# A hybrid attention, SSM and mixture-of-experts step on one core: coefficient tables and rotations built at other places on VectorE, GELU in four blocks, two of five output tiles summed on TensorE

## The reference

```
h = rmsnorm(x);  q, k, v, u = split(h @ w_in)
a = sink_attention(q, k, v)                 # window 128; streams read a cache
abar, bbar = discretise(a_re, a_im, log_dt, b)      # complex, 32 groups x 64 states
h_t = abar * h_(t-1) + bbar u_t;  y = Re(C h) + d u
y = gelu(y);  y = y * sigmoid(y @ w_glu + b_glu)
x = x + concat(rmsnorm(a), rmsnorm(y)) @ w_out
f = rmsnorm(x);  x = x + sum over 2 chosen of 32 experts of gate * swiglu_e(f)
out = rmsnorm(x, g_final)
```

## Time and profile before

| | |
|---|---|
| median of 3 runs | 891.31 us (889.7 to 893.34) |
| the profiled execution | 890.42 us |
| its span, first to last instruction | 888.2 us |
| outside the span | 2.2 us |
| mean granted TensorE clock | 0.918 |
| PE, DVE, ACT, POOL busy share | 86%, 36%, 24%, 19% |

### The profile page before, as it was taken

How to read it: one execution, slowest core, us unless ns; L and a number is a source line. 1 busy time by engine, 2 the same in 40 slices (tenths; PEclk the granted TensorE clock), 3 DMA queues, 4 the chain that set the end, 5 groups by cost and what they waited for, 6 DMA issues and landing times.

```text
span 888.2 us, 15231 instructions
## 1 busy us (share of the span) xinstructions
PE 766.0 (86%) x5066; PEld 482.6 (54%) x5067; DVE 319.6 (36%) x754; ACT 214.0 (24%) x445; POOL 168.3 (19%) x380
## 2 busy tenths in 40 slices
PE   5999977799999993899998878888999999999840
PEld 3555555557554553566664444445666666666520
DVE  3478699760225335222211111111222122222117
ACT  4000244500422221122221211212222222222113
POOL 2006003300002001322222212222222222222110
PEclk9999988995789995899998999999999999999885
DMA  8202153180772439799999999999999968999955
GB/s 350 84 0 100 41 61 68 14 225 10 227 308 67 170 152 397 280 419 414 418 416 420 416 419 417 419 419 418 418 413 397 416 251 349 417 419 416 416 208 247
DMA packets 59617, 255.76 MB, mean 288 GB/s; under 512 B 19850, under 2 KB 22794, under 8 KB 36368
## 3 DMA queue, kind: packets, MB, share of 16 engines
q1 hardware_dynamic: 52560, 242.86, 69.8%
q0 software_dynamic: 6240, 11.46, 3.5%
q10 hardware_dynamic: 768, 0.72, 0.2%
HBM read 241.38 MB, written 22.30 MB: 297 GB/s over the span
## 4 chain that ended last, share of the span: by engine, by line
PE 59%; DMA 17%; SPq 10%; DVE 8%; ACT 3%; issue 2%; POOLq 0%; POOL 0%; DVEq 0%; ACTq 0%
PE pair L957 15%; PE pair L979 12%; DMA slot<-in_w_exp_down 10%; PE pair L753 7%; PE pair L616 6%; SPq L334 4%; PE pair L958 3%; DMA kv_row<-in_w_exp_down 3%; DMA slot<-in_w_in_qkv 2%; SPq L337 2%; PE pair L858 2%; PE pair L931 2%; PE pair L678 2%; PE pair L617 2%; SPq L325 2%
## 5 line engine op out<-in xcount | busy, mean ns | idle before, releaser
L958 PE MATMUL pair<-slot,probs 128*64 128x256 f32 x800 | 178.6, 382 | 0.0
L1603 DVE TENSOR_TENSOR sums<-iota_t,sums 128x640 bf16<-128x640 f32 x38 | 32.0, 841 | 286.4 <-POOL sums L547 280.3
L957 PE MATMUL pair<-slot,probs 128*64 128x256 f32 x576 | 129.1, 383 | 5.9 <-issue 3.3
L979 PE MATMUL pair<-slot,sums 128*64 128x512 f32 x400 | 100.7, 648 | 16.1 <-DMA slot<-in_w_exp_down 12.9
L958 PEld LDWEIGHTS pair<-slot,probs 128*64 128x64 f32 x800 | 110.2, 138 | 0.0
L957 PEld LDWEIGHTS pair<-slot,probs 128*64 128x64 f32 x576 | 79.4, 139 | 45.0 <-issue 12.9
L616 PE MATMUL pair<-reg_h,slot 128*128 128x512 f32 x160 | 84.0, 607 | 4.0 <-DMA slot<-in_w_in_qkv 2.2
L958 PE MATMUL pair<-reg_f,probs 128*64 128x256 f32 x384 | 84.9, 380 | 0.0
L531 POOL DMA_INDIRECT y_scr<-sums,y_now x40 | 42.8, 1070 | 189.8 <-ACT sums L1175 132.3
L523 POOL DMA_INDIRECT probs<-hf_scr,row_u x38 | 40.1, 1056 | 202.8 <-DMA y_scr<-sums,y_now 106.0
L957 PE MATMUL pair<-reg_h,probs 128*64 128x256 f32 x352 | 77.9, 379 | 0.3 <-DMA slot<-in_w_exp_up 0.3
(11 more groups left out here) (367 smaller groups left out, 1089.6 us busy)
## 6 DMA issues: line engine op xcount, KB each, us to landing
slot<-in_w_exp_up SPq DMA_DIRECT2D x22, 2048.0 KB, 24.2
slot<-in_w_exp_down SPq DMA_DIRECT2D x44, 1024.0 KB, 24.5
slot<-in_w_exp_gate SPq DMA_DIRECT2D x16, 2048.0 KB, 27.4
reg_f<-in_w_exp_up SPq DMA_DIRECT2D x10, 2048.0 KB, 25.4
reg_h<-in_w_exp_gate SPq DMA_DIRECT2D x8, 2048.0 KB, 26.8
reg_x<-in_w_exp_gate SPq DMA_DIRECT2D x8, 2048.0 KB, 28.6
reg_h<-in_w_exp_down SPq DMA_DIRECT2D x10, 512.0 KB, 23.1
reg_f<-in_w_exp_down SPq DMA_DIRECT2D x10, 512.0 KB, 21.8
```

Source lines behind the costliest of these rows:

```text
L957: pe.matmul(gu[j][0:TT], lhs, gate_w[g][:, h, c, out], start=n == 0, stop=n == KD - 1)
L958: ins = pe.matmul(gu[j][TT:P], lhs, up_w[q][:, h, c, out], start=n == 0, stop=n == KD - 1)
L979: ins = pe.matmul(yp[TT * h:TT * h + TT], hid_t[:, k, :], down_w[q][k][:, 512 * h:512 * h + 512], start=k == 0, stop=k == KH - 1)
L1603: tt(sel, iota_t[:].unsqueeze(1).to_broadcast([P, NT, P]), place_of[:, 0].unsqueeze(2).to_broadcast([P, NT, P]), ALU.is_equal)
```

## The change

Five edits, all in the order or the place of work; what is computed stays the same.

1. **VectorE, early.** `proj_out(0)` to `proj_out(5)` are moved later in VectorE's program, and the powers and step tables so come earlier. `out_table(0)` is made right after the step tables (in two parts, with `probs` as scratch), and `rotations(0, 4)` right after `masked(0)`.
2. **VectorE, in the loop.** `rotations(4, 6)` moves from turn 1, behind `masked(3)`, to turn 0, ahead of `proj_out(7)`. `out_table(1)` moves from turn 3 to turn 1, behind `masked(3)`, in four parts with 1024 columns of `slot[0]` as scratch. `out_table(0)` leaves turn 2. That scratch is later written by `bp_copy`, so ScalarE waits for `out_tab_done` ahead of those copies.
3. **Streams on VectorE.** The input halves (`stream_in`) of groups 0 and 1 run ahead of the output half of group 0, and so on.
4. **GELU.** ScalarE runs both remaining stream copies, `pt_copy(9)` and `pt_copy(10)`, ahead of GELU, and GELU in four blocks of 640 columns; TensorE's gate product waits for one block at a time.
5. **Tail.** VectorE makes four diagonal 128x128 matrices of the gates. TensorE adds tiles 1 and 3 in PSUM: the identity times the residual, plus each diagonal times its `got` rows. ScalarE and VectorE then read these two tiles from PSUM. VectorE adds tiles 0, 2 and 4 as before; the steps stand in another order.

The core of the diff:

```diff
-            proj_out(0)
...
             for n, (x, y) in {2: (1, 1), 3: (2, 1), 4: (2, 2), 5: (4, 1), 6: (4, 2), 7: (4, 3), 8: (4, 4)}.items():
                 cmul(power(n), power(x), power(y), (pv(12), pv(14)))
-                if n == 5:
-                    proj_out(2)
+                if n == 3:
+                    proj_out(0)
+            proj_out(1)
...
             dve.wait_ge(s["in_small"], 48)
+            out_table(0, probs[:].rearrange("p b n -> p (b n)"))
+            proj_out(5)
             masked(0)
+            rotations(0, 4)
             kv_rows()
...
+                if n == 0:
+                    rotations(4, 6)
                 if n < 3:
                     proj_out(7 + n)
                 if n + 2 < 8:
                     masked(n + 2)
-                if n == 0:
-                    rotations(0, 4)
-                elif n == 1:
-                    rotations(4, 6)
+                if n == 1:
+                    out_table(1, spare)
+                    dve.sem_inc(s["out_tab_done"], 1)
...
-                if n in (2, 3):
-                    out_table(n - 2)
```

```diff
+            stream_in(0)
+            stream_in(1)
+            stream_out(0)
+            stream_in(2)
+            stream_out(1)
+            stream_out(2)
...
-            act.wait_ge(s["y_in"], 16)
-            act.activation(y_g, y_t, ACT.Gelu_apprx_tanh).then_inc(s["gelu_done"], 1)
             pt_copy(9)
             pt_copy(10)
+            act.wait_ge(s["y_in"], 16)
+            for b in range(GB):
+                act.activation(y_g[:, b], y_t[:, b], ACT.Gelu_apprx_tanh).then_inc(s["gelu_done"], 1)
```

```diff
+            pe.wait_ge(s["diag_done"], 1)
+            pe.wait_ge(s["resid_back"], 16)
+            for i in by_pe:
+                for h in range(2):
+                    pe.matmul(by_pe[i][:, 512 * h:512 * h + 512], ident[:], resid[:, i, 512 * h:512 * h + 512],
+                              start=True, stop=False)
+            for n, i in enumerate(by_pe):
+                pe.wait_ge(got_in[i], 16)
+                for h in range(2):
+                    for k in range(2):
+                        ins = pe.matmul(by_pe[i][:, 512 * h:512 * h + 512], dg[:, n, k],
+                                        got[i][:, k, 512 * h:512 * h + 512], start=False, stop=k == 1)
+                ins.then_inc(s["summed"], 1)
...
             dve.wait_ge(s["resid_back"], 16)
-            for i in range(NT):
+            add_rows(0)
+            mean_square(0)
+            final_norm(0)
+            for i in range(2, NT, 2):
                 add_rows(i)
-                if i >= 1:
-                    final_norm(i - 1)
+                mean_square(i - 1)
+                final_norm(i - 1)
                 mean_square(i)
-            final_norm(NT - 1)
+                final_norm(i)
```

More of the change, by code:

```diff
@@ L102, in build @@
         x_t = reg_h[:].rearrange("p (k t) -> p k t", k=KD)
-        out_tmp = [reg_h[:, 2048 * i:2048 * i + 2048].rearrange("p (r t c) -> p r t c", r=R, t=T) for i in range(2)]
+        spare = slot[0][:, 2560:3584]
         states = reg_h[:, 0:2560].rearrange("p (r i n) -> p r i n", r=R, i=2)
@@ L208, in build @@
         down_w += [[reg_h[:, 4096:5120], reg_f[:, 4096:5120], probs_t[:], kv_f[:, 0:D]]]
+        pp = [ctx.enter_context(nc.psum_tensor(f"pair{i}", [P, 2, 512], F32)) for i in range(4)]
+        pp_sum = [pp[1][:].rearrange("p b n -> p (b n)"), pp[2][:].rearrange("p b n -> p (b n)")]
         xrow = probs[:, 0, 0:512]
@@ L1304, in _ @@
             dve.sem_inc(s["bbar_done"], 1)
-            proj_out(3)
+            proj_out(2)
             def step_table(i):
@@ L1348, in out_table @@
                           for n in range(2)]
-                c1, c2 = out_tmp
-                tt(c1, (cr, ci)[i], ar, ALU.mult)
-                step(tt(c2, (ci, cr)[i], ai, ALU.mult))
-                step(tt(out_tab[:, :, i], c1, c2, (ALU.add, ALU.subtract)[i]))
+                n = tmp.shape[1] // (2 * R * GC)
+                c1, c2 = tmp.rearrange("p (x r t c) -> p x r t c", x=2, r=R, t=n)[:, 0], \
+                    tmp.rearrange("p (x r t c) -> p x r t c", x=2, r=R, t=n)[:, 1]
+                for t in range(0, T, n):
+                    part = lambda x: x[:, :, t:t + n]
+                    tt(c1, part((cr, ci)[i]), part(ar), ALU.mult)
+                    step(tt(c2, part((ci, cr)[i]), part(ai), ALU.mult))
+                    step(tt(part(out_tab[:, :, i]), c1, c2, (ALU.add, ALU.subtract)[i]))
             def kv_rows():
@@ L1497, in _, with stream_in @@
             op_out(1)
-            for j in range(3):
+            def stream_in(j):
                 nb = min(3, NB - 3 * j)
```

36 lines of the change are left out of this document (22 added, 14 removed).

## The result

| | before | after |
|---|---|---|
| median of 4 runs each | 890.85 us (889.70 to 893.34) | 881.37 us (880.52 to 882.36) |
| ratio, 95% interval | | 0.9877 (0.9846 to 0.9907) |
| the profiled execution, its span | 890.42, 888.2 us | 880.52, 878.8 us |
| repeated beside 29 runs of before: mean of 10 | 893.15 us | 884.81 us, ratio 0.9905 (0.9876 to 0.9934) |

Forecast were 886.3 us and a range of 883.8 to 890.5; the change brought more than that, 9.5 us at first and 8.3 when repeated. The ratios in this document are the recorded ones; they are not the quotients of the medians or means beside them, and differ from these by up to 0.2%. I cut both traces at five points that stand in every kernel: four starts in TensorE's program, `scores(0)`, the first product of `out_project`, the first sample scores and the first gate (GLU) product, and VectorE's first add of the tail.

The account below looks back on a forecast made before the run. TensorE held 59% of the end's chain, DMA 17%, VectorE 8%; front -2.5, GELU -0.5 and tail -2.0 made -5.0 on 890.42, 885.4, or 886.3 us against the median, range 883.8 to 890.5.

Parts of the forecast that it names:

- Streams and GELU: Sample products: TensorE's 0.51 us wait for copies behind GELU goes, -0.5 us, bounds -0.5 and +0.5; reordered halves bring nothing.
- The cover that I named for GELU behind the copies: At the gate product: GELU's first block ready at 248.9 us, ahead of TensorE's need, with 1 us of cover.
- Front: Mixing part up to scores(6): moved tables and rotations remove the wait ahead of turn_probs(3), -2.5 us, bounds -4.2 and -0.5.
- The bound of -4.2: Largest gain allowed ahead of scores(6), with TensorE's clock staying full through weighted(1) and chunk_sums.
- `kv_rows` no longer waits for TensorE: Sign of a wrong forecast in VectorE's early part: it would mean that part is overfull; about 1 us of waiting was expected left.
- `ssm_out`'s clock changed: Sign of a wrong forecast: TensorE's clock in the SSM's output products was expected to stay as before.
- From `scores(6)` at 149.30 on, each engine waits as before, shifted: Step behind the early mixing part: what is gained by scores(6) is kept, with later waits unchanged.
- Tail: From VectorE's first add to the end: two pairs of adds go to TensorE, -2.0 us, bounds -2.15 and +2.2.
- Rival (b): Tail: TensorE stays at 1.2 GHz, 2.08 us a product, tail ends 2.2 us later than before; 890.5 us or less, chance 0.12.
- (a): Front: GpSimd's later clearing meets masked(5) and costs it 3.3 us, so the front yields nothing; 888.8 us, chance 0.14.
- (d): Front: clock falls in gaps at 121 to 130 us, stays low to chunk_sums' end; +6.2 us, 897.5, chance 0.05.
- The rule on transposes: Turning in the front: transposes don't count as TensorE activity in the same way, so the clock would stay low through it.

Follow-up runs that it names:

- after_again: The changed kernel run once more with no edit; mean 884.81 us, ratio 0.9905 to the kernel before.
- front_only: The kernel before with only the moved tables, rotations and early output drains on VectorE; mean 889.93 us, ratio 0.9976.
- tail_only: The kernel before with only the new tail, two tiles summed by TensorE; mean 890.97 us, ratio 0.9972.
- no_streams: The changed kernel with GELU and VectorE's sample order put back as before; mean 886.76 us, ratio 0.9920 to the kernel before.
- no_front: The changed kernel with tables, rotations and early drains put back as before; mean 886.64 us, ratio 0.9935 to the kernel before.
- best1: The changed kernel with tables, rotations and drains as before and GpSimd's conv_w clearing moved behind the states; mean 885.28 us, ratio 0.9925 to the kernel before.
- clear_later: The kernel before with one line moved, GpSimd clearing conv_w behind the states; mean 891.74 us, ratio 0.9991.

## Why the prediction was wrong

By the means of four traces each the change brought 7.1 us where the sum had 5.0: 2.1 more in streams and GELU, 0.5 more in the tail, 1.2 less in the front, and 0.7 in stages that it doesn't act on.

**Streams and GELU, the step that failed.** "-0.5 us", with bounds of -0.5 and +0.5, was the wait of one execution, 0.51 us, taken for the size of the thing. The wait is what is left between two moving times: `y_t` from DRAM plus 3.1 us for GELU and two copies, and TensorE's arrival, which depends on its clock. It was short in that trace since TensorE ran at 0.57 over 233 to 241 us. Over nine traces it ran from none to 4.95 us, and the clock stayed low longer behind the long ones: some 7 us behind waits of up to 0.5 us, some 10 behind those of about 2 to 3, some 14 behind the two above 4. The part is worth 2.6 us in the mean of these traces, 7.3 in the one pair with the full clock. No rival held this, and the earlier trace rows with the clock of 233 to 241 us would have pointed to it: `out_project`'s last part would be 1.9 us shorter at the full clock (3.60 in the trace of after, not 5.46), the landing where it was, hence some 1.9 us more wait. The cover that I named for GELU behind the copies held, 0.9 us in `after_again` where I said 1: no block made TensorE wait.

**Launch, not in the sum.** -2.48 us of the recorded pair are the two executions' own, which is chance. The first comparison's interval, 877.1 to 882.6 us, lies below the range; the repeated one, put on the same 890.85 us, gives 882.4, and its interval, 879.8 to 885.0, reaches into it. So it is the stages, more than the time, that show the wrong step.

**Front: the steps right, the last one wrong.** `out_table(0)` took 7.7 us in its new place (7.5 said), `rotations(0, 4)` 5.4 (5.4). Counted from `scores(0)`, `project(8)` came 0.78 us late (0.85), the turning 1.84 late (1.7 on its own), `turn_probs(3)` 1.36 early (1.5), `scores(6)` 3.07 early (2.5). The clock at 138 us stayed up, and `weighted(1)` took 1.8 us (2.0); `chunk_sums` gained nothing, as a new wait of 0.96 us for ScalarE stands in it. The bound of -4.2 is more than its terms, 1.5 and 2.4, which make 3.9. Two of the signs that I had named for a wrong forecast came. `kv_rows` no longer waits for TensorE: the 1.8 us of waiting that I left ahead of the first two projections are gone, the early part is just full, and `project(7)` is 0.07 us late. And `ssm_out`'s clock changed, the +2.02 us of the third stage. The step that fell is "From `scores(6)` at 149.30 on, each engine waits as before, shifted": low stretches appeared at about 152 and in most traces at 170 us, and 1.3 us were left at `out_project` in the mean, none in `front_only`. The time of `front_only`, -2.9 us with an interval from -4.7 to +0.4 (the ratio's bounds on 892.8), doesn't tell more.

**Tail: right, 0.5 us too careful.** It takes 19.1 us against 21.6 in the four traces of after, in `tail_only` and in `no_streams`: -2.5, where I said -2.0 and -2.15 at best. My chain of small steps ended 19.43 us behind the first add, 0.33 too long by rounding, and I took off 0.15 for a late tile. Rival (b) is real but small: with the clock at 0.50 under the first of these products the tail took 20.2 us, in `no_front` and `best1`, still 1.4 less than before.

**The other rivals.** (a) didn't come: the clearing, from 132.69 us, met `masked(5)`, whose large operation took 1.23 us as elsewhere, while the scalings of `unit_out(3)` took 1.14.

```profile
125.12 1.14 DVE L1446 TENSOR_SCALAR probs<-probs,sm 128x256 f32<-128x256 f32 x4
...
132.69 3.52 POOL L483 MEMSET slot<- 128x4096 f32 x1 [61.92 <-PE pair L638]
133.77 1.23 DVE L1457 TENSOR_TENSOR slot<-pair,reg_f 128x1024 f32<-128x1024 f32 x1 [7.51 <-PE pair L706]
```

`clear_later` shows that the 3.3 us were the clearing's. The port rule of the Trainium skill ("SBUF — State Buffer", "Who interferes with whom") agrees with the trace on both. (d) didn't come either: granted were 0.56 over 130 to 132 us and 1.00 over 132 to 134, after some 4 us of transposes alone.

```profile
130.00:132.00 2.00, 2.00 (x12) 1.49 (x10) 0.00 (x0) 1.30 (x3) 0.00 (x0) 0.56 1.39 116
132.00:134.00 2.00, 2.00 (x16) 1.45 (x16) 0.23 (x1) 1.15 (x2) 1.31 (x1) 1.00 1.40 119
```

The rule on transposes of the Trainium skill ("TensorE: Matmul & The Clock Gate", "Part 4: PE-mode transpose") would have kept the clock low there; the measurement decides.

**Open.** It stays open why the low stretches come where they do, and whether the first four times of after (880.52 to 882.36) all had the full clock over the sample products: four of the ten later ones lay at 880.08 to 882.75, and the one trace of such a time had it. How the parts add up isn't settled below 1 us either: alone they give 7.4 us by their means, left out singly 1 to 2 us each (886.76, 886.64 and 885.86 less after's 884.81, in other comparisons).

## What to carry to other kernels

A short wait right behind a slow stretch of the waiting engine is not small; work out when the other side arrives, and what the wait becomes if the stretch runs at its full rate. Put work that waits for DRAM behind, not ahead of, copies that another engine needs, in every in-order queue. A gain at one point of a stage that TensorE holds isn't a gain at its end: read a point of the program some 30 us later, in more than one execution, before the gain goes into the sum.
